# A hybrid attention and gMLP layer on one core: the copies of the turned probabilities one step earlier

## The reference

```
h      = RMSNorm_pre(x)
q,k,v,gate_a,u,v_b,gate_b,mg_a,mg_b = split(h @ w_in)
o_a    = sliding_window_attention(q, k, v, sinks, rel_bias)   # 16 heads of 64, 2 kv heads, window 128
y_a    = (o_a * silu(gate_a)) @ w_branch_a
o_b    = spatial_gating(gelu(u), gelu(v_b), ...)              # causal chunks of 128
y_b    = (o_b * silu(gate_b)) @ w_branch_b
out    = (sigmoid(mg_a) * y_a + sigmoid(mg_b) * y_b) @ w_out
x      = x + RMSNorm_post(out)
```

## Time and profile before

| | |
|---|---|
| median of three runs | 937.08 us (934.45 to 937.41) |
| profiled execution | 935.18 us, span 933.4 us |
| TensorE busy | 891.1 us, 95% |
| VectorE busy | 620.2 us, 66% |
| GpSimd busy | 537.3 us, 58% |
| ScalarE busy | 507.7 us, 54% |
| granted TensorE clock | 0.997 of full |
| DMA | 139.29 MB, mean 149 GB/s |

### The profile page before, as it was taken

The page is one execution under the profiler, slowest core; times in us unless marked ns, Lnnn a source line. Parts: engine busy times, 40 slices in busy tenths (PEclk is TensorE's granted clock), DMA queues, the critical chain, the costliest instruction groups (busy, mean ns, idle before and its releaser), DMA issues.

```text
span 933.4 us, 12475 instructions
## 1 busy us (share of the span) xinstructions
PE 891.1 (95%) x4204; PEld 740.2 (79%) x4204; DVE 620.2 (66%) x1135; ACT 507.7 (54%) x982; POOL 537.3 (58%) x395
## 2 busy tenths in 40 slices
PE   9999999999999998899999989999999999999997
PEld 8888888877777776677777778878888888888886
DVE  6776794544454553445454567879769968989968
ACT  6654356756757574657667674434353534434553
POOL 3564237687888776687788867645444042042226
PEclk9999999999999999999999999999999999999999
DMA  8885746444444457555444454552359560235004
GB/s 299 198 198 159 249 134 182 140 114 129 111 125 117 134 137 158 175 122 146 119 121 108 121 180 134 173 154 91 113 182 382 188 219 22 93 133 225 0 1 181
DMA packets 199184, 139.29 MB, mean 149 GB/s; under 512 B 91320, under 2 KB 164048, under 8 KB 198992
## 3 DMA queue, kind: packets, MB, share of 16 engines
q1 hardware_dynamic: 196880, 135.05, 48.7%
q10 hardware_dynamic: 2240, 3.43, 1.0%
HBM read 98.06 MB, written 43.54 MB: 152 GB/s over the span
## 4 chain that ended last, share of the span: by engine, by line
PE 54%; POOL 23%; issue 9%; DVE 4%; ACT 4%; DMA 3%; SPq 1%; POOLq 0%; DVEq 0%; ACTq 0%
PE acc L1032 13%; PE acc L1204 11%; PE acc L885 9%; POOL w_lo L1816 8%; PE ps_m L1204 7%; PE ps_t L1204 7%; POOL pt_pack L1859 4%; POOL pt_prev L1864 3%; DMA raw<-in_w_in 3%; PE acc L975 2%; POOL sums L1881 2%; POOL sums L1882 2%; POOL gate L1873 1%; PE ps_m L1072 1%; POOL sums L1888 1%
## 5 line engine op out<-in xcount | busy, mean ns | idle before, releaser
L1032 PE MATMUL acc<-mv,w_hi 128*128 128x512 f32 x1344 | 346.7, 391 | 1.2 <-ACT ev L1408 0.7
L1032 PEld LDWEIGHTS acc<-mv,w_hi 128*128 128x128 f32 x1344 | 247.5, 188 | 48.8 <-ACT w_hi L1363 1.1
L1032 PE MATMUL acc<-mv,w_lo 128*128 128x512 f32 x672 | 180.8, 391 | 0.0
L1816 POOL TENSOR_TENSOR w_lo<-sums,w_hi 128x1024 fp32r<-128x1024 f32 x48 | 117.2, 2444 | 71.4 <-ACT w_hi L1370 42.2
L1032 PEld LDWEIGHTS acc<-mv,w_lo 128*128 128x128 f32 x672 | 126.7, 189 | 27.5
L1816 POOL TENSOR_TENSOR w_lo<-raw,w_hi 128x1024 fp32r<-128x1024 f32 (+1 forms) x48 | 94.4, 1967 | 37.1 <-ACT w_hi L1363 27.8
L1572 ACT ACTIVATE soft<-soft,neg_max 128x129 f32<-128x129 f32 x128 | 50.5, 396 | 92.6 <-DVE neg_max L2134 68.0
L1204 PE MATMUL acc<-right,left 128*128 128x512 f32 x432 | 98.7, 389 | 0.0
L1204 PEld LDWEIGHTS acc<-right,left 128*128 128x128 f32 x432 | 81.0, 188 | 17.2 <-DVE left L2194 0.4
L1859 POOL TENSOR_TENSOR pt_pack<-soft,pt_pack 128x512 fp32r<-128x512 f32 x32 | 44.8, 1401 | 52.2 <-ACT pt_pack L1589 52.2
L885 PE MATMUL acc<-mv 128*128 128x512 f32 x288 | 69.5, 395 | 0.0
(11 more groups left out here) (282 smaller groups left out, 1664.5 us busy)
## 6 DMA issues: line engine op xcount, KB each, us to landing
raw<-in_w_in SPq DMA_DIRECT2D x56, 512.0 KB, 5.6
prob_d<-soft SPq DMA_DIRECT2D x32, 256.0 KB, 3.4
soft<-prob_d SPq DMA_DIRECT2D x128, 64.0 KB, 2.7
ht_d<-sums SPq DMA_DIRECT2D x8, 512.0 KB, 4.8
mix_d<-mix_b SPq DMA_DIRECT2D x8, 512.0 KB, 3.9
ga_d<-gate SPq DMA_DIRECT2D x16, 256.0 KB, 3.6
tb<-tb_d SPq DMA_DIRECT2D x4, 1024.0 KB, 5.4
ub<-mix_d SPq DMA_DIRECT2D x7, 512.0 KB, 3.4
```

Of the source, the lines that this page charges most:

```text
L1032: ins = nc.tensor.matmul(bank, (w_lo if y == 2 else w_hi)[:, left + k * P:left + (k + 1) * P], right[:, (OPW if y == 1 else 0) + k * HALF: ...
L1816: nc.gpsimd.tensor_tensor(w_lo[:, c], src, w_hi[:, c].bitcast(f32), ALU.subtract).then_inc(wlo_ok, 1)
```

## The change

ScalarE's `turned_hi` moves from the end of step 3c+7 (behind the step's evictions) to step 3c+6, inside `attend`, so ahead of that step's `after`. It goes past one step's attention work and the `after` of two steps. For couple 3 (step 15, step 1 of the next pair) it also stands ahead of the next pair's normalising and exponentials of that step, since the older pair comes first. GpSimd's low half and mask move from step 3c+8 to step 3c+7. What SyncE, TensorE and VectorE do, and every wait, is unchanged.

```diff
@@ ScalarE, attend(p, k)
                     nc.scalar.activation(o_tmp[64:128, :], o[0:64, 256:512], ACT.Copy).then_inc(otmp_ok, 1)
+                for c in couple_at(k, 6):
+                    turned_hi(4 * p + c)
@@ ScalarE, the loop over steps
                     for at in attention_all(n, s):
                         attend(*at)
                     after(n, s)
-                    for p, k in attention_all(n, s):
-                        for c in couple_at(k, 7):
-                            turned_hi(4 * p + c)
@@ GpSimd, attend(p, k)
-                for c in couple_at(k, 8):
+                for c in couple_at(k, 7):
                     j = 4 * p + c
                     pool.wait_ge(turn_hi, j + 1)
```

## The result

| | before | after |
|---|---|---|
| median | 935.77 us (932.98 to 937.41, 4 runs) | 901.33 us (900.03 to 903.22, 4 runs) |
| profiled execution | 935.18, span 933.4 | 901.79, span 900.0 |
| TensorE busy | 891.1 us, 95% | 886.7 us, 99% |

The ratio is 0.9637 [0.9604, 0.9669]: faster, by 34 us where 41 were forecast from the median. The profiled executions differ by 33.4 us.

The account below looks back on a forecast made before the run. The prediction held TensorE's waits for GpSimd's mask, an in-order chain, to be the bound. Waits 37.5 plus keys 4.3 gave 41.8 us off 935.18, so 893.4; 895.3 as a median, rounded up to 896, range 890 to 912.

Parts of the forecast that it names:

- What bounds the kernel: Value matmuls: TensorE waits 31.3 us in 23 places for GpSimd's mask, an in-order chain; no other engine is full.
- What one wait costs: TensorE at the value matmuls: each wait costs 0.27 us more than its gap, 37.5 us for all.
- The four couples: Masks of couples 0 to 3 in each head pair: ready 2.6, 2.9, 3.1 and 4.7 us early, every wait gone.
- L1859 beside VectorE: GpSimd's low half on a shared read interface: moved pieces could each lose 0.4 us; the sum left unchanged.
- The keys: End of the fourth head pair: TensorE's 3.02 us wait falls to 0.4, the clock holds, 4.3 us won.
- the evictions behind late data: Pair with the reloads: weights late from memory can delay L1408; covered by rounding 895.3 up to 896.
- Behind the attention stretch TensorE is busy all the time: After the attention stretch: the change touches nothing, so a microsecond won in the stretch is won at the end.
- The sum: Whole kernel: 37.5 + 4.3 = 41.8 us off the profiled execution of 935.18.
- evictions late: Rival at L1422 and L1408: TensorE waits 0.7 us at two places in eight pairs, 11 us, time 907; chance 0.09.
- GpSimd late: Rival at couples 0 and 1: masks just in time or late by half today's waits, time 914; chance 0.07.

Follow-up runs that it names:

- Experiments 1: The changed kernel with only ScalarE's copy moved, GpSimd's low half and mask left at step 3c+8: 923.34 us, ratio 0.9863.
- 3: The changed kernel with ScalarE's copy one position later, in `attend` of step 3c+7, still ahead of that step's evictions: 911.49 us, ratio 0.9741.
- experiments 5 and 6: The kernel before and the changed kernel, in that order, each without the reload of keys and values for the second kv head: 928.72 us and 898.15 us.
- Experiment 7: The changed kernel with SyncE's two loads of the gates four steps later, behind the weight loads: 898.4 us, ratio 0.96.
- experiment 8: The changed kernel with the gates' loads four steps later and the second kv head's values behind the weight loads in two halves: 895.94 us, ratio 0.9574.
- experiment 10: The changed kernel with ScalarE's high half of couple 1 made four times in a row instead of once: 910.27 us, ratio 0.9739.
- experiment 2: The kernel before with only GpSimd's low half and mask moved to step 3c+7, ScalarE's copy left in place: 960.37 us, ratio 1.0268.

## Why the prediction was right, and where it was short

The time on record is 896, measured are 901.33; the direction, the mechanism and the range hold.

- **What bounds the kernel: right.** With the waits for the mask gone, TensorE is busy in all of a pair. No other engine took its place.
- **What one wait costs: right.** A pair is 50.22 - 45.61 = 4.61 us shorter; the three gaps are 3.84 and three restarts at 0.27 are 0.81, together 4.65. Experiments 1 and 3 need the same 0.27 for their sums.
- **The four couples: right** to a tenth: 2.65, 2.85, 3.11 and 4.76 us of margin against 2.6, 2.9, 3.1 and 4.7. ScalarE waits 0.82 us for the values at couple 3's L1589 (300.51), and that moves nothing. GpSimd's only wait in front of a low half is couple 0's 2.64.
- **L1859 beside VectorE.** It fell from 1400 to 1290 ns a piece in the pair, so the moved pieces meet VectorE less, not more, than in the earlier trace rows.
- **The keys: right.** 0.4 us of wait was forecast and 0.08 is left (at 341.88), and the clock holds. That is 2.94 of wait and 1.7 of clock, 4.6 us, against 4.3; experiments 5 and 6, which are coarser, give 3.9 for the whole reload.
- **The step that was short: the evictions behind late data.** The prediction named it ("can delay L1408") and gave it 0.7 us by rounding. It measures, around the reload, 0.29 + 1.63 + 0.84 = 2.8 us and three restarts, and at 577 us, where the prediction did not look at all, 2.8 net of what was there before. Experiment 7 gets 2.9 us back from the one and experiment 8 another 2.5 from the other, and lands at 895.94. The sign of it lies in the rows of before: L1363 waited 5.77 us for the same weight at 612.05. That wait did not shrink when the rest got faster, it grew to 7.39. The rows divide the 1.62: ScalarE is ready 35.78 us earlier than before (570.50 against 606.28), SyncE issues the weights only 34.69 earlier (566.48 against 601.17), which is 1.09, and they take 0.53 longer to land, with an issue of 6.11 us instead of 5.51. Why SyncE gets there no sooner was not followed back. I had gone through the waits that TensorE has now, not through the waits of ScalarE for DMAs that were covered.
- **"Behind the attention stretch TensorE is busy all the time": wrong in a detail.** The two gaps of 0.70 and 0.55 were there, and in their place a longer one came.
- **The sum.** With 4.6 us for the keys instead of 4.3 the forecast is 42.1 us. Less 4.15 for the other five gaps that are left, 1.35 for their restarts at 0.27 and 2.8 at 577 us, 33.8 should be won; by the spans 33.4 are. A restart costs about as much at a product as at the values: in the fifth pair, with two such gaps, TensorE is busy for 46.12 us where it is 45.61 in an undisturbed one, 0.26 each.

The rival *evictions late* has the right place (L1408 and L1422), in a few places and not in each pair. Its own reason, L1589 waiting for the reads back with the evictions behind it, is true of the gap of 0.29; for the 1.63, the 0.84 and the 2.31 it is another, the late weights. In all ScalarE waits 10.3 us for reads back in L1589, five times, up to 3.3, and nearly all of it is covered. In an undisturbed pair there is only the 0.82 for the values, as forecast. The rival *GpSimd late* is refuted by the margins; experiment 3 shows that with the copy one position later it would have come true at couples 0 and 1, with waits of 0.3 us.

## What to carry to other kernels

When a piece is moved ahead in an in-order queue, ask whether what feeds it comes earlier too. Here the consumer alone, moved ahead while its producer stayed, blocked its own queue and what stood behind it (23 us lost), the producer alone gave 14, and both 34. When a wait is to go, list also the waits for DMAs that the helping engines have under its cover, with what stands in front of each in the issuing queue; here these were the next bound, and moving two loads that could wait behind the weights was worth 5.4 us. Price a wait of TensorE with its restart, and one of two microseconds or more with the clock behind it.

## What the runs showed of the hardware

TensorE's granted clock after a wait. In all twelve profiled runs, from 150 to 650 us, none of the 32 waits of 1.5 to 1.96 us was followed by a lower clock. Of the 27 of 2.02 us or more 21 were, by a stretch at 0.50 (1.2 GHz) that began between 0.8 us before the wait's end and 1.6 us after it, and 6 were not. No such stretch came without a wait of this size. A fall cost 1.5 to 1.7 us, once 3.0. So a wait just over two microseconds can cost nearly twice itself. Length alone does not decide: the kernel before waited 2.92 us until 397.25 and experiment 10 waited 2.45 until 530.65, and the clock stayed:

```profile
399.30:401.30 2.00, 2.00 (x11) 1.64 (x10) 1.90 (x7) 1.40 (x5) 2.00 (x3) 1.00 0.85 272
```

```profile
532.50:534.50 2.00, 2.00 (x14) 1.74 (x13) 1.97 (x4) 1.29 (x2) 0.63 (x1) 1.00 0.88 87
```

A low half beside VectorE's gate product was slow again, in experiment 2:

```profile
273.55 0.69 DVE L2109 SCALAR_TENSOR_TENSOR gate<-ev 128x512 f32<-128x512 f32 x1
...
273.66 1.69 POOL L1859 TENSOR_TENSOR pt_pack<-soft,pt_pack 128x512 fp32r<-128x512 f32 x1 [3.85 <-ACT pt_pack L1589]
```

It is 1.69 us long where the pair's other three took 1.29 to 1.30, as in the earlier trace rows. The Trainium skill, in "SBUF — State Buffer", section "Who interferes with whom", says that a VectorE instruction with two SBUF inputs, as this one is, and a GpSimd instruction that reads SBUF share a read interface; the low half is 0.4 us longer beside it in both traces, which agrees.
